# Gates of the embedding: the tile before is finished ahead of the eviction

## What is computed

```python
h = h + m.astype(h.dtype)
g = jax.nn.sigmoid((rms_norm(h, ple_norm[i]) @ ple_w_gate[i]).astype(F32))
h = h + (g * (p[i] @ ple_w_proj[i]).astype(F32)).astype(h.dtype)
```

## Time and profile before

| | us |
|---|---|
| time, median of 3 runs (4171.75 to 4172.13) | 4172.12 |
| the profiled execution, its own time | 4171.61 |
| its span in the trace | 4169.8 |
| PE busy | 3807.0 (91%) |
| DVE busy | 2742.4 (66%) |
| ACT busy | 2084.3 (50%) |
| POOL busy | 603.4 (14%) |

### The profile page before, as it was taken

One profiled execution on the slowest core, in us unless ns is written; L12 is line 12 of the kernel. 1 busy time (PEld: TensorE's weight loads), 2 busy tenths in 40 slices (PEclk: granted clock), 3 DMA queues, 4 the chain that ended last, 5 costly groups with the idle time before them and its releaser, 6 DMA issues.

```text
span 4169.8 us, 79401 instructions
## 1 busy us (share of the span) xinstructions
PE 3807.0 (91%) x29682; PEld 3626.3 (87%) x29682; DVE 2742.4 (66%) x4186; ACT 2084.3 (50%) x3218; POOL 603.4 (14%) x564
## 2 busy tenths in 40 slices
PE   7999999988899986899999999799898977999997
PEld 6999999877789986898999999798888867999996
DVE  6777666566666765666677765787777766554454
ACT  5555555555545546555555545454444443343342
POOL 1011012100002201122011112222222230100000
PEclk9999999999999998999999999899999988999998
DMA  5555544444444432445555545344344432444442
GB/s 218 192 209 202 192 172 171 173 173 171 171 162 172 174 131 101 153 170 188 207 193 201 202 170 182 121 152 152 143 152 143 152 112 87 152 168 147 153 164 88
DMA packets 93586, 681.72 MB, mean 163 GB/s; under 512 B 10401, under 2 KB 10529, under 8 KB 11169
## 3 DMA queue, kind: packets, MB, share of 16 engines
q1 hardware_dynamic: 92880, 676.75, 45.1%
q0 software_dynamic: 464, 1.64, 0.1%
HBM read 676.25 MB, written 2.10 MB: 163 GB/s over the span
## 4 chain that ended last, share of the span: by engine, by line
PE 61%; DVE 16%; ACT 9%; issue 8%; POOL 4%; DVEq 1%; ACTq 0%; DMA 0%; POOLq 0%; SPq 0%
PE g L375 18%; PE g L376 17%; PE g L377 17%; DVE w_lo L1350 6%; ACT w_hi L861 4%; POOL scratch L2140 3%; PE g L435 1%; PE g L434 1%; PE norm_bank L388 1%; ACT scratch L908 1%; ACT scratch L907 1%; PE turn_bank L414 1%; DVE scratch L1847 1%; PE rope_bank L407 1%; DVE scratch L1411 1%
## 5 line engine op out<-in xcount | busy, mean ns | idle before, releaser
L1350 DVE TENSOR_TENSOR w_lo<-w_raw,w_hi 128x1024 fp32r<-128x1024 f32 x1280 | 1579.0, 1239 | 949.8 <-ACT w_hi L861 947.4
L861 ACT ACTIVATE w_hi<-w_raw 128x1024 fp32r<-128x1024 f32 x1280 | 1320.6, 1053 | 1247.1 <-PE g L377 1227.1
L375 PE MATMUL g<-p_hi,w_hi 128*128 128x256 f32 x4624 | 1344.9, 291 | 65.1 <-DVE p_lo L1380 16.9
L376 PE MATMUL g<-p_lo,w_hi 128*128 128x256 f32 x4624 | 1321.7, 286 | 0.0
L377 PE MATMUL g<-p_hi,w_lo 128*128 128x256 f32 x4624 | 1320.6, 286 | 0.0
L375 PE MATMUL g<-q_hi,w_hi 128*128 128x256 f32 x3472 | 1003.8, 289 | 58.5 <-DVE q_lo L1921 14.8
L376 PE MATMUL g<-q_lo,w_hi 128*128 128x256 f32 x3472 | 991.0, 285 | 9.4 <-issue 9.4
L377 PE MATMUL g<-q_hi,w_lo 128*128 128x256 f32 x3472 | 990.5, 285 | 0.0
L375 PEld LDWEIGHTS g<-p_hi,w_hi 128*128 128x128 f32 x4624 | 899.4, 195 | 83.0 <-DVE w_lo L1350 37.9
L376 PEld LDWEIGHTS g<-p_lo,w_hi 128*128 128x128 f32 x4624 | 901.4, 195 | 1.0
L377 PEld LDWEIGHTS g<-p_hi,w_lo 128*128 128x128 f32 x4624 | 900.6, 195 | 0.0
(11 more groups left out here) (367 smaller groups left out, 3984.7 us busy)
## 6 DMA issues: line engine op xcount, KB each, us to landing
w_raw<-in_slots SPq DMA_DIRECT2D x640, 1024.0 KB, 4.8
h<-in_x SPq DMA_DIRECT2D x1, 2048.0 KB, 10.8
out_h<-h SPq DMA_DIRECT2D x1, 2048.0 KB, 6.3
sq<-in_p POOLq DMA_DIRECT2D x4, 256.0 KB, 2.9
con<-in_consts SPq DMA_DIRECT2D x1, 878.0 KB, 5.0
scratch<-in_distance POOLq DMA_DIRECT2D x1, 576.0 KB, 4.1
vec<-in_vecs SPq DMA_DIRECT2D x1, 383.0 KB, 3.1
scratch<-in_positions SPq DMA_DIRECT2D x1, 128.0 KB, 6.3
```

Of the source, the lines that this page charges most:

```text
L375: pe.matmul(g, wh, hi[:, k], start=n == 0, stop=False)
L376: pe.matmul(g, wh, lo[:, k], start=False, stop=False)
L861: act.activation(w_hi[k % SPLIT][:, cols], raw[k % RAW][:, cols], ACT.Copy).then_inc(hi_ready, 1)
L1350: dve.tensor_tensor(w_lo[k % SPLIT][:, cols], raw[k % RAW][:, cols], w_hi[k % SPLIT][:, cols], SUB).then_inc(lo_ready, 1)
```

## The change

In the gates only. VectorE finishes tile j-1 and takes its low part ahead of the eviction of tile j (before, finish(j-1) and low(j-2) came behind the second weight half). ScalarE's tail of j-1 moves between the two weight halves, and the sigmoid of j comes behind the second one. GpSimd adds the square of j-1 ahead of the clamp of j. No instruction is added or removed.

```diff
@@ ScalarE, gates @@
                 for j in range(8):
-                    tick()
-                    sigmoid(zg[:, j % 2], clamped, c.next("clamped"))
+                    c.next("slot")
+                    act.wait_ge(half_used, c.next("half"))
+                    hi_ahead(0)
                     if j:
                         finish(j - 1)
+                    act.wait_ge(tile_done, c.next("tile"))
+                    hi_ahead(1)
+                    sigmoid(zg[:, j % 2], clamped, c.next("clamped"))
                 finish(7)
@@ VectorE, gates @@
                 for j in range(8):
                     begin()
+                    if j > 0:
+                        finish(j - 1)
+                        low(j - 1)
                     g = take()
                     dve.tensor_tensor(zg[:, j % 2], g, rstd[:], MUL).then_inc(tile_taken, 1)
                     lo_half(1)
-                    if j > 0:
-                        finish(j - 1)
-                    if j > 1:
-                        low(j - 2)
                 finish(7)
-                low(6)
                 low(7)
@@ GpSimd, gates @@
                 for j in range(8):
+                    if j and not last:
+                        add_squares(j - 1, half == 0 and j == 1)
                     c.next("tile")
                     clamp(zg[:, j % 2], zg[:, j % 2])
-                    if j and not last:
-                        add_squares(j - 1, half == 0 and j == 1)
```

## The result

The changed kernel takes 4201.07 us (median of 6 runs, 4195.2 to 4202.22), the kernel before beside it 4171.93 (4168.0 to 4172.47). The ratio is 1.0069, with a 95% interval of 1.0056 to 1.0082. It is slower by 29 us; 4198 was forecast, in a range of 4186 to 4252.

A forecast was written before the change was run, and what follows sets the result against it. The prediction took a cross-engine ring of 6.44 us per gate tile as the bound, TensorE a little under it. Layers 0 to 2 add 24.0 us, layer 3 1.7: +25.7 on 4171.61 gives 4198 us, range 4186 to 4252.

The forecast's parts named there:

- The ring: Gates, layers 0 to 2: closed chain across engines from eviction to next eviction, 6.44 us before, forecast 6.95 us.
- The steps put in: VectorE, between the weights' low part and the eviction: finish(j-1), rounding wait and low(j-1) add 0.46 + 0.54 + 0.60 + 0.42 = 2.02 us.
- The race at the clamp: GpSimd's clamp against VectorE's second weight low part: clamp starts first by 0.15 us and lasts 0.84 instead of 1.64.
- Rival 1: Gates: the low part beats the clamp, interval 8.18 us, total 4250 us; chance 0.20.
- the working: Gate stages, eight-tile halves: two halves cost +9.9 us in layers 0 to 2 and +3.3 in layer 3, before the ends.
- The ends: Eighth and sixteenth tile of a layer: clamp over at 1.45 instead of 2.25 us behind the eviction, -1.6 us.
- TensorE's pace: Gates: layer 3's interval of 5.80 us, taken as TensorE's bound if the ring became shorter.
- rival 2: Gates: finish and low fall into VectorE's idle time, ring 4.93 us, TensorE bounds at 5.80, total 4148 us; chance of faster 0.04.
- Point of decision: Gates' ring: to get faster, 2.02 us put in must be under 0.71 + 0.80 us taken out.

The follow-up runs named there:

- the halves together again: Changed kernel with ScalarE's two weight halves adjacent again, tail of j-1 behind them, ahead of the sigmoid of j: 4248.51 us, 1.019 of the kernel before.
- the one with one line moved: Kernel before, with VectorE's low part of the second weight half moved behind finish(j-1): 4131.29 us, 0.991 of the kernel before.
- the low part off the stretch: Changed kernel with low(j-1) on VectorE moved behind the second weight half: 4196.34 us, 1.0066 of the kernel before.
- finish first: Changed kernel with VectorE ordered finish(j-1), first low half, eviction of j, low(j-1), second low half: 4133.23 us, 0.9917 of the kernel before.

## Why the prediction was right, point by point

**The ring.** Forecast 6.95 us, measured 6.96. The steps put in, each by itself: multiply to add 0.45 (0.46 said), add to rounding 0.55 (669.26 to 669.81; 0.54 said), rounding to low part 0.61 (0.60), low part to eviction 0.41 (0.42). For the rounding to low part I had bounds of 0.53 and 0.70 and took the middle; it lies there because VectorE goes on 0.10 behind a rounding of 0.51, not 0.03 as behind a sigmoid.

**The race at the clamp.** Forecast: clamp first by 0.15, 0.84 long. Measured: first by 0.14 and 0.85 long, in 14 of 16 tiles of each stage of layers 0 to 2; the first of a half is at 1.64, as said. The margin was as thin as it looked. Rival 1's interval (8.18) is what the two tiles with a late clamp show above (8.23), and the halves together again make the low part win everywhere, two moved lines on ScalarE away from the changed kernel. That this run's 4248.5 lies so near to the 4250 of rival 1 is chance: its interval is 7.93, and layer 3, which rival 1 left alone, takes 102.9 us from first to last eviction instead of 91.7. The bounds of the prediction held the low part's start and the eviction, but not a clamp that GpSimd starts 0.3 late; that the changed kernel has none was not foreseen.

**The rest of the sum.** First to last eviction of a stage grew by 9.4 in layer 0 (98.8 to 108.2), 9.6 and 9.5 in layers 1 and 2 (98.7 to 108.3, 98.7 to 108.2); the working gives 9.9 - 0.8 = 9.1. In layer 3 it grew from 90.4 to 91.7, 1.4, where the working gives 3.3 - 0.8 = 2.5: its interval is 5.85 and not 5.92, because the step from high to low part, taken as 1.14 from the earlier trace rows, is 1.08 once the two high halves no longer stand together. Together 29.9 against 29.8; the nearness is partly luck, for layers 0 to 2 are 1.3 over the working and layer 3 is 1.1 under it. The ends give 1.1 back in each of layers 0 to 2, as said (layer 0: 11.0 from the last eviction to the next stage's first, now 10.0).

**Three us more than forecast.** Of the 30.5 us on the span the gates and their ends explain about 26. The rest, some 4.6 with both signs (+1.8 ahead of the first gates, -1.4 between those of layers 0 and 1, +1.8 ahead of those of layer 2, +3.1 ahead of layer 3's, -0.6 behind them), lies in stages in which no instruction differs. Up to layer 3 it goes with TensorE's granted clock, for which my sum had no term. A window of 30 us before the gates of layer 3, at about the same work, in the kernel before, the changed one and the one with one line moved (columns as above; the last three are granted clock, DMA share and GB/s):

```profile
2430.00:2460.00 30.00, 27.62 (x209) 26.67 (x209) 15.46 (x26) 13.36 (x26) 1.55 (x2) 0.95 0.35 122
...
2460.00:2490.00 30.00, 27.62 (x195) 26.67 (x195) 14.78 (x22) 11.38 (x18) 1.55 (x2) 0.89 0.27 90
...
2394.00:2424.00 30.00, 27.21 (x213) 26.12 (x214) 16.43 (x29) 14.30 (x27) 1.55 (x2) 1.00 0.38 137
```

From the last eviction of layer 2 to the first of layer 3 the clock stood at 0.50, the 1.2 GHz level, for 10.2, 17.1 and 0 us in these three, and the stretch took 622.3, 624.2 and 619.8 us. The first gate eviction of layer 0 comes at 654.1 to 654.8 us in the three profiles with no such time ahead of it, at 654.9 to 656.1 in the four with 3.4 us, at 658.4 in the one with 10.2, though all kernels are the same up to there. Behind layer 3's gates the sign does not fit (3.6 us more of it, 0.6 us shorter). Why the clock falls in one execution and not in another was not tried.

**What was wrong: TensorE's pace.** I read layer 3's 5.80 us as TensorE's. It was the ring's: without rounding and square, 6.44 - 0.71 and 0.07 more between high and low part give 5.80, and with the short clamp the same layer has intervals of 4.93 and then 5.76. TensorE's own pace is 5.76. It did not matter for the forecast, but rival 2 (4148; a real kernel of that kind, finish in the idle time, takes 4133) and my expectation of 4145 for the one moved line rest on it. Between the two profiled executions that line saves 40.1 us of span where I had 27. The gates save 30.6 of them and not 25: with the clamp at 0.85 layer 3 runs from 2507.7 to 2596.7, 89.0 instead of 90.4, and layers 0 to 2 gain 9.8 each instead of 8.3. The gaps between the stages save 7.4 and not 2. Part of this is at the ends, where layers 0 and 2 gain 1.5 each (11.0 to 9.5 from the last eviction to the next stage's first), and the rest is of the size of the scatter named above. By the medians of the runs side by side it saves 36.5.

**Point of decision.** 2.02 put in against 0.71 + 0.80 taken out was the right account: 6.96 - 6.44 = 0.52 us an interval.

## What to carry to other kernels

Before moving work "into idle time", write the ring of one iteration down, across all engines, and see whether the place you move it to lies between two steps of the ring; an idle time ahead of an instruction is not an idle time behind it. When one wait is taken away, look at once for the step that is queued behind it on the next engine: the low part off the stretch gave nothing until GpSimd's order went with it. And look at instructions that are longer in one place than in another: the one that paid most here was a clamp twice as long as it need be, cured by one line.

## What the runs showed of the hardware

The clamp on GpSimd (one input, 128x256) takes 0.85 us alone, and is held back by a two-input subtraction of 128x1024 on VectorE that started earlier: it ends 1.92 us behind the subtraction's start whether it starts 0.28 or 0.59 behind it, and 2.12 behind it where the subtraction is itself stretched by 0.20 (halves together). The reverse costs little: a subtraction that starts 0.10 us behind the clamp takes 1.38 instead of 1.22 (two tiles of the run with one line moved), one 0.14 behind 1.33, one 0.18 behind 1.30, and an add 0.17 behind takes 0.51 instead of 0.42. A subtraction 0.24 behind takes 1.23, and one 0.47 behind was not stretched at all. From these I estimate that GpSimd lets go about 0.25 us after its start, long before its 0.85 are over. How long VectorE holds on seems to go with the size: with a low part of a tile (128x256, both inputs in SBUF) 0.28 ahead of it the clamp took 0.90 (finish first, second halves). A multiply of the same size with one input in PSUM, 0.28 ahead (672.12 and 672.40), kept its usual 0.41 and left the clamp at 0.85.
